# Convolution layer's two projections by seven half-size products per pair of column blocks, on one core

## What is computed

```
h = rms_norm(x, norm_g) @ w_in                  # w_in: 2048 x 8192
b_gate, c_gate, hx, z = split(h, 4)
u = c_gate * hx
conv = causal width-3 convolution of u, per channel
y = (b_gate * conv * silu(z)) @ w_out           # w_out: 2048 x 2048
x = x + y
```

## Time and profile before

| | |
|---|---|
| time, median of 3 runs | 2505.37 us (2504.8 to 2506.09) |
| span of the profiled execution | 2504.4 us |
| PE busy | 2451.6 us (98%) |
| DVE busy | 1500.7 us (60%) |
| ACT busy | 1020.4 us (41%) |
| first product of `conv_in` | at 33.12 us |
| first matmul of `project_and_score` (block 0) | at 1004.63 us |
| first matmul of its block 1 | at 1018.52 us |

### The profile page before, as it was taken

How to read it: one execution, slowest core, us unless ns; L and a number is a source line. 1 busy time by engine, 2 the same in 40 slices (tenths; PEclk the granted TensorE clock), 3 DMA queues, 4 the chain that set the end, 5 groups by cost and what they waited for, 6 DMA issues and landing times.

```text
span 2504.4 us, 51142 instructions
## 1 busy us (share of the span) xinstructions
PE 2451.6 (98%) x20963; PEld 2152.2 (86%) x20963; DVE 1500.7 (60%) x1682; ACT 1020.4 (41%) x1848; POOL 341.4 (14%) x134
## 2 busy tenths in 40 slices
PE   8999999999999999999999999999999989899998
PEld 7999999999999999999999989999999833355555
DVE  5675556566666334455699887777677567533311
ACT  4111112111112223677745468777645445531111
POOL 4423332332321011000000000000000013300000
PEclk9999999999999999999999999999999999999999
DMA  5333332333332433322577777787889899999997
GB/s 159 85 84 93 91 84 84 84 84 86 99 84 69 122 106 108 104 99 90 189 266 268 254 260 257 248 295 271 289 292 307 296 372 416 402 345 374 388 410 299
DMA packets 361063, 520.54 MB, mean 208 GB/s; under 512 B 17033, under 2 KB 289810, under 8 KB 342418
## 3 DMA queue, kind: packets, MB, share of 16 engines
q1 hardware_dynamic: 304578, 461.55, 53.4%
q10 hardware_dynamic: 56192, 56.45, 6.5%
q0 software_dynamic: 128, 0.26, 0.0%
HBM read 483.46 MB, written 34.75 MB: 207 GB/s over the span
## 4 chain that ended last, share of the span: by engine, by line
PE 86%; DVE 4%; ACT 4%; DMA 3%; issue 1%; SPq 1%; POOL 0%; ACTq 0%; DVEq 0%; POOLq 0%
PE psum L117 25%; PE psum L1311 17%; PE psum L125 13%; PE psum L1319 8%; PE psum L2015 7%; PE psum L1362 4%; PE psum L2094 4%; DMA w_raw<-in_w_in_b_dram 2%; DVE h_keys_turned L1254 1%; PE psum L2073 1%; ACT w_raw L1075 1%; PE psum L1327 1%; PE psum L2054 1%; DMA w_raw<-in_w_in_a_dram 1%; PE psum L1341 1%
## 5 line engine op out<-in xcount | busy, mean ns | idle before, releaser
L1311 PE MATMUL psum<-x_hi,w_hi 128*128 128x272 f32 x2048 | 433.4, 293 | 0.8 <-ACT work L133 0.8
L117 PE MATMUL psum<-x_hi,w_hi 128*128 128x272 f32 x2048 | 426.7, 289 | 2.2 <-DVEq L451 2.2
L117 PE MATMUL psum<-x_lo,w_hi 128*128 128x272 f32 x2048 | 425.8, 289 | 0.0
L1311 PE MATMUL psum<-x_lo,w_hi 128*128 128x272 f32 x2048 | 424.9, 289 | 0.0
L1311 PEld LDWEIGHTS psum<-x_hi,w_hi 128*128 128x128 f32 x2048 | 321.2, 189 | 17.7 <-issue 17.6
L117 PEld LDWEIGHTS psum<-x_hi,w_hi 128*128 128x128 f32 x2048 | 321.1, 189 | 2.7 <-issue 2.3
L1311 PEld LDWEIGHTS psum<-x_lo,w_hi 128*128 128x128 f32 x2048 | 321.0, 188 | 0.0
L117 PEld LDWEIGHTS psum<-x_lo,w_hi 128*128 128x128 f32 x2048 | 320.5, 188 | 0.0
L1254 DVE STREAM_TRANSPOSE h_keys_turned<-h_ring 128x1024 f32<-128x1024 f32 x256 | 300.0, 1215 | 21.3 <-DMA h_ring<-in_cache_k_dram 12.3
L404 POOL TENSOR_TENSOR w_raw<-w_raw,params 128x2048 f32<-128x2048 f32 x63 | 243.4, 3864 | 504.5 <-DMA w_raw<-in_w_in_a_dram 504.5
L1319 PE MATMUL psum<-x_hi,w_lo 128*128 128x272 f32 x2048 | 284.1, 294 | 0.0
(11 more groups left out here) (222 smaller groups left out, 2987.5 us busy)
## 6 DMA issues: line engine op xcount, KB each, us to landing
h_ring<-in_cache_k_dram SPq DMA_DIRECT2D x256, 512.0 KB, 6.4
ring<-in_cache_v_dram SPq DMA_DIRECT2D x128, 1024.0 KB, 7.7
w_raw<-in_w_in_a_dram SPq DMA_DIRECT2D x64, 1024.0 KB, 6.2
w_raw<-in_w_kv_dram SPq DMA_DIRECT2D x16, 2048.0 KB, 13.2
w_raw<-in_w_in_b_dram SPq DMA_DIRECT2D x15, 2048.0 KB, 8.9
w_raw<-in_w_out_a_dram SPq DMA_DIRECT2D x16, 1024.0 KB, 5.6
wo_raw<-in_w_out_b_dram SPq DMA_DIRECT2D x32, 512.0 KB, 7.8
ring<-in_w_out_b_dram SPq DMA_DIRECT2D x16, 1024.0 KB, 6.6
```

The lines of the kernel that those rows point to most:

```text
L117: pe.matmul(out[:, g, 0:GT], m.WH[s][:, k * P:(k + 1) * P], x[:, k * T + g * GT:k * T + (g + 1) * GT], start=(k == 0 and x is xh), stop=Fa ...
L1311: pe.matmul(psum[n % 2][:, g, 0:GT], m.WH[n % 2][:, k * P:(k + 1) * P], x[:, k * T + g * GT:k * T + (g + 1) * GT], start=(k == 0 and x is ...
```

## The change

One function, `seven_products`, takes the place of `read_inputs`, `conv_in` and `conv_out`. It takes two column blocks at a time, so 40 steps (n = 0 to 39; 32 for `w_in`, 8 for `w_out`). A step's weights are cut into four quarters A11, A12, A21, A22 (even or odd row tiles, first or second block; 8 tiles of 128x128 each), and the activations into quarters likewise (even or odd channel tiles, first or second group of 272 columns). By Strassen's scheme (in Winograd's form) the four quarters of the result come of seven products of half size in place of eight, numbered mm = 0 to 6, with the left sides A11, S1, S2, A12, S3, A22, S4, where S1 to S4 are sums of quarters. A product is 16 matmuls with the high half of its left side and 8 with the low half, each 128x128 by 272 columns, all into one PSUM bank. The first product's bank is copied by ACT into another bank (`seed`) and two later products add to that; ACT and DVE take the quarters out (`take_u2`, `take_u3`, `take_quarter`, `gather`).

Per step, DVE makes the four sums (1024 columns each) and seven low halves, ACT seven high halves. SP loads the four quarters apart, 512 KB each in pieces of 512 bytes.

The seven right sides are the quarters of x and their sums. In step 0 they are made from x, which is now multiplied by the norm weight on ACT while it is turned (so the weights of `w_in` are no longer scaled), and raw x is stored to memory. For `w_out` the right sides are made from y, step by step; they are stored to memory in `conv_extras` (they don't fit beside those of x) and loaded again during step 31 by `load_right`: 14 transfers of 128 rows of 7616 bytes, on ACT's queue. From step 32 to 39, x is added back, split, and the split halves are stored, and during step 39 loaded again by `load_x1` into `x_hi` and `x_lo`, but for the last two tiles: six transfers of 128 rows of 8704 bytes and two of 4352. The first two weight blocks of the next stage are loaded by SP after product 3 of step 39 (2 MB in pieces of 512 bytes). The gate's SiLU is one ACT instruction. The additions of squares in the last 8 steps stay on POOL. All loops are written out.

DVE at the start, before: for each of the first channel tiles the low half of x, and for odd tiles the sum of squares.

The diff, cut:

```diff
--- before.py
+++ after.py
-def project_hi(pe, m, s, out, xh, xl, waits={}):
...
-def project_lo(pe, m, s, out, xh):
...
-def load_next(sp, m, following, lo_ready, raw_in, n):
...
+IN_STEPS, OUT_STEPS = 2 * KT, KT // 2
+STEPS = IN_STEPS + OUT_STEPS
+TICKS = STEPS * PRODUCTS
+LEFT = ["A11", "S1", "S2", "A12", "S3", "A22", "S4"]
+RIGHT = [0, 4, 1, 2, 3, 5, 6]
+BANK_OF = [0, 2, 1, 0, 1, 6, 2]
...
+OPENS = (0, 1, 5)
...
+        return {"S2": 0, "S3": 1, "S1": 4, "S4": 5 + n % 2, "A21": 8, "A22": (9, 7)[n % 2], "A11": 10, "A12": 11}[name]
...
+            def load(name, n):
+                kind, i, part = columns_of(n)
+                w, col = (d["w_in_a"][0], CONV_IN_COLS[part] + 2 * i * P) if kind == "in" else (d["w_out_a"][0], 2 * i * P)
+                if name == "A21" and n:
+                    sp.wait_ge(s_ready, 4 * (n - 1) + 3)
+                if name == "A22" and n >= 2:
+                    sp.wait_ge(product_done, PRODUCTS * (n - 2) + 6)
+                if name == "A22" and n == 1:
+                    sp.wait_ge(xt_ready, KT)
+                if name == "A11" and n:
+                    sp.wait_ge(product_done, PRODUCTS * (n - 1) + 1)
+                if name == "A12" and n:
+                    sp.wait_ge(product_done, PRODUCTS * (n - 1) + 4)
+                sp.sem_inc(granted, 1)
+                odd, right = int(name[2]) - 1, int(name[1]) - 1
+                sp.dma_start(arena.left(name, n).rearrange("p (k c) -> p k c", k=EDGE),
+                             w.rearrange("(k two p) c -> two p k c", two=2, p=P)[odd][:, :, col + right * P:col + (right + 1) * P]
+                             ).then_inc(w_in[name], 16)
...
+            sp.wait_ge(s_ready, 4 * STEPS)
+            sp.wait_ge(product_done, PRODUCTS * LAST + 4)
+            for s in range(SLOTS):
+                sp.sem_inc(granted, 1)
+                sp.dma_start(tiles(m.RAW[s][:, :]), w_block(w, cols + s * P)).then_inc(q_in[s], 16)
+            for s in range(SLOTS):
+                sp.wait_ge(q_in[s], 48 - 16 * s)
...
+                if k == 0:
+                    act.wait_ge(par_ready, 1)
+                act.wait_ge(raw_ready, k + 1)
+                if k % 2 == 0:
+                    both = arena.plain[0][:, :].rearrange("p (o x) -> p o x", x=RW)[:, 4:8:3, :]
+                    act.activation(both[:, :, i * GT:(i + 1) * GT], xt, ACT.Copy, scale=gain).then_inc(gx_ready, 1)
+                else:
+                    act.activation(arena.right_plain(2)[:, i * GT:(i + 1) * GT], xt[:, 0, :], ACT.Copy, scale=gain)
+                    act.activation(arena.right_plain(6)[:, i * GT:(i + 1) * GT], xt[:, 1, :], ACT.Copy, scale=gain).then_inc(gx_ready, 1)
+                after(act, sq_used, k - 1)
+                act.activation(grouped(sq[k % 2][:, :]), xt, ACT.Square).then_inc(sq_ready, 1)
+                if k >= 1:
+                    x_raw_store(k - 1)
...
+            def split_high(q):
+                if q >= TICKS:
+                    return
+                n, mm = divmod(q, PRODUCTS)
+                left_landed(act, LEFT[mm], n)
+                after(act, product_done, q - 3)
+                act.activation(arena.left_high(q), arena.left(LEFT[mm], n), ACT.Copy).then_inc(hi_ready, 1)
...
+                act.activation(arena.right(order, 0), arena.right_plain(order), ACT.Copy).then_inc(right_high, 1)
...
+                act.wait_ge(product_done, PRODUCTS * n + 1)
+                if n == 0:
+                    act.wait_ge(seed_bits, 1)
+                if n >= 2:
+                    act.wait_ge(product_done, PRODUCTS * (n - 2) + 5)
+                act.activation(bank(n, 2), bank(n, 0), ACT.Copy).then_inc(act_took, 1)
...
+                    act.activation(b1, b2, ACT.Silu).then_inc(act_gate, 1)
...
+            def load_right(mm):
+                order = RIGHT[mm]
+                act.wait_ge(product_done, PRODUCTS * (IN_STEPS - 1) + mm + 1)
+                if mm == 0:
+                    act.wait_ge(y_out, 80 * (EDGE - 1))
+                entry = [0, 4, 1, 5, 3, 6, 2][order]
+                for low in range(2):
+                    act.dma_start(arena.right(order, low)[:, 0:(EDGE - 1) * GT].bitcast(F32),
+                                  st.YS[low, entry].rearrange("p i t -> p (i t)")[:, 0:(EDGE - 1) * GT]).then_inc(right_in[mm], 16)
...
+                if n == LAST and mm in (1, 3, 4):
+                    load_x1({1: 0, 3: 1, 4: 2}[mm])
+                if n == LAST and mm == 6:
+                    load_x1(3)
...
+            def load_x1(order):
+                act.wait_ge(product_done, PRODUCTS * LAST + RIGHT.index(order) + 1)
+                if order == 3:
+                    x1_stored(act, OUT_STEPS - 2)
+                k0, k1 = 4 * order, (4 * order + 4 if order < 3 else KT - 2)
+                for low, x in enumerate((XH, XL)):
+                    act.dma_start(x[:, k0 * T:k1 * T].bitcast(F32), st.X1S[low][:, k0 * T:k1 * T]).then_inc(right_in[order], 16)
...
+            act.wait_ge(q_in[1], 32)
+            for k in range(KT):
+                wk = m.RAW[1][:, k * P:(k + 1) * P]
+                ins = act.activation(wk, wk, ACT.Copy, scale=m.PAR[:, following[2] + k:following[2] + k + 1])
+            ins.then_inc(q_scaled, 1)
+            act.wait_ge(q_scaled, 2)
+            act.wait_ge(product_done, PRODUCTS * LAST + 4)
+            act.activation(m.WH[0][:, :], m.RAW[0][:, :], ACT.Copy).then_inc(q_high, 1)
...
+                    done = k // 4 * 3
+                    dve.wait_ge(gx_ready, k + 1)
+                    dve.tensor_tensor(t1, b12, b11, ALU.subtract).then_inc(t_step, 1)
+                    dve.wait_ge(t_step, done + 1)
+                    dve.tensor_tensor(t2, b22, t1, ALU.subtract).then_inc(t_step, 1)
+                    dve.tensor_tensor(b12, b22, b12, ALU.subtract)
+                    dve.wait_ge(t_step, done + 2)
+                    dve.tensor_tensor(t4, b21, t2, ALU.subtract).then_inc(t_step, 1)
...
+            def gather(n, mm):
+                dve.wait_ge(product_done, PRODUCTS * n + (2, 6, 7)[mm])
+                if mm == 0:
+                    dve.wait_ge(act_took, 4 * n + 4)
+                    dve.tensor_tensor(quarter(n, 1, 1), u3, bank(n, 1), ALU.add).then_inc(dve_took, 1)
+                if mm == 1:
+                    dve.tensor_tensor(quarter(n, 1, 0), u3, bank(n, 5), ALU.add).then_inc(dve_took, 1)
+                if mm == 2:
+                    dve.tensor_tensor(quarter(n, 0, 1), u2, bank(n, 6), ALU.add).then_inc(dve_took, 1)
...
+                if n == 0 and mm < 5:
+                    right_lows(2 + mm)
+                if n + 1 < STEPS and mm >= 3:
+                    (sum_1, sum_2, sum_3, sum_4)[mm - 3](n + 1)
...
+            dve.wait_ge(q_high, 1)
+            dve.wait_ge(product_done, PRODUCTS * LAST + 5)
+            dve.tensor_tensor(m.WL[0][:, :], m.RAW[0][:, :], m.WH[0][:, :].bitcast(F32), ALU.subtract).then_inc(q_low, 1)
+            gather(LAST, 2)
+            add_x(OUT_STEPS - 1)
+            x1_lows(OUT_STEPS - 1)
...
+                for k in range(EDGE):
+                    if n == IN_STEPS and k == EDGE - 1:
+                        pe.wait_ge(right_high, PRODUCTS + mm + 1)
+                        pe.wait_ge(yl_ready, 2 * (EDGE - 1) + mm + 1)
+                    for low in range(2):
+                        pe.matmul(to, wh[:, k * P:(k + 1) * P], arena.right(RIGHT[mm], low)[:, k * GT:(k + 1) * GT],
+                                  start=(mm in OPENS and k == 0 and low == 0), stop=False, skip_group_check=True)
+                pe.wait_ge(lo_ready, q + 1)
+                for k in range(EDGE):
+                    last = pe.matmul(to, wl[:, k * P:(k + 1) * P], arena.right(RIGHT[mm], 0)[:, k * GT:(k + 1) * GT],
+                                     start=False, stop=(k == EDGE - 1), skip_group_check=True)
+                last.then_inc(product_done, 1)
...
@@ build @@
-                one = read_inputs(nc, m, d, st, (d["w_in_a"][0], CONV_IN_COLS[0:2]), block)
...
-                conv_in(nc, m, d, st, (d["w_out_a"][0], 0), one, block)
-                conv_out(nc, m, d, st, head_weights(d, "q"), one, block)
+            one = seven_products(nc, m, d, st, Arena(plain, rounded), extra, extra_r, head_weights(d, "q"), block)
```

1131 lines of the change are left out of this document (680 added, 451 removed).

## The result

The changed kernel takes **2447.95 us** (median of 4 runs, 2445.57 to 2451.49) beside 2505.68 us (2504.8 to 2506.09) for the kernel before on the same chip: a ratio of **0.9773, 95% interval 0.9759 to 0.9787**. The gain is 57.7 us, where 42 was forecast. (The 2505.37 us above are the median of the first three of the kernel before's four runs here.) The profiled execution has a span of 2446.5 us.

What follows compares the result with a forecast made beforehand. PE was taken as bound by the first layer's matmul count. From 2504.4 us: -120.6 matmuls, -2 a wait, +31.6 start, +18 and +31 the two turns give a span of 2462.4; forecast 2463 us, range 2424 to 2497.

Steps and rivals of the forecast that it cites:

- What bounds the kernel: In the first layer PE is bound by its number of matmuls; each one removed is worth its pitch.
- an eighth of the matmuls: Over the 40 steps 960 matmuls go, at 0.1256 us each: -120.6 us; no change of pitch taken.
- The steady steps hide their new work: In steps of 21.09 us, DVE's and ACT's added work stays hidden under PE: no cost.
- 90%, under PE: DVE's work over four steps of `w_in`: 76 of 84.4 us, so hidden under PE.
- It fits, by 0.4 us: At a third step's start, ACT's seed copy ends at 5.6 us, before product 2 begins at 6.0.
- The start: Before steady steps, DVE and ACT hand over in turn: first product at 56 us, step 0 ends at 89; +31.6 us.
- The turn to the second projection: Around steps 31 and 32, left side A12 lands late beside large right-side packets: +16 us, +18 with PE's clock.
- Products 5 and 6 find their right sides landed: At the turn to the second projection, these products of step 32 wait for no right sides: no cost.
- 2 us for PE's clock: After the wait at the second projection, PE starts again at 1.2 GHz: about 2 us.
- The turn to the next stage: After step 39, weight blocks land late behind x's transfers; block 1 starts 45.3 us after step 39: +31 us.
- turn 1: The turn to the second projection, steps 31 and 32: forecast at +18 us.
- turn 2: The turn to the next stage, from the last step's start to block 1: forecast at +31 us.

Runs made afterwards that it cites:

- e6: Changed kernel with 24 more matmuls in each step's last product, as many as before the change (projection values wrong): 2567.5 us.
- e12: Changed kernel with one more DVE instruction per product in steps 1 to 31, which nobody waits for: 2491.12 us.
- e5: Changed kernel with POOL adding only 16 of 544 columns of each tile's squares at the start (norm wrong): 2443.68 us.
- e7: Changed kernel with the 14 loads of right sides on SP's queue, in one row with the left sides in due order: 2450.47 us.
- e9: As e7, with the left side A12 of step 32 loaded ahead of the third pair of right sides: 2447.7 us.
- e8: Changed kernel with x1's loads and the next stage's weight blocks in due order on SP's queue, and ACT rounding the first block before scaling the second: 2434.94 us.
- e1: Changed kernel with the second projection's right sides padded in memory, so loads go in packets of 1088 bytes instead of 7616: 2458.03 us.
- e10: Changed kernel with the edits of e8 and e9, and the start's sums made after the next four tile copies: 2433.36 us.
- e3: Changed kernel with ACT rounding the next stage's first weight block before scaling the second: 2446.68 us.

## Why the prediction was right

**The range and the sign held, and the forecast was 15 us too slow.** Three of its sums are right in their mechanism and near in size, one is near in size by luck, and the largest miss lies where it had no term. Point by point:

- *What bounds the kernel* and *an eighth of the matmuls*: right. 3.01 us per product, 0.1255 per matmul, no price for one bank (as the earlier trace rows had pointed to). e6 gives the count of matmuls as the gain of the steps.
- *The steady steps hide their new work*: right, at 21.09 us, and durations as worked out. The transposes of the last rows, 0.2 us in every fourth step, were not counted. The sentence "90%, under PE" was made over four steps (85% measured, 71.3 of 84.4); e12 shows that the hand-overs and the fullest steps decide. The line that mattered was "It fits, by 0.4 us": the copy behind `first_tap` was forecast to end at 5.6 us of the third step and ends at 5.4, and it is the place where e12 first makes PE wait. In a kernel a little fuller the 90% would have misled.
- *The start*, 31.6 forecast and 28.9 measured: the mechanism is right (DVE and ACT in turn, rounds of 10.0 us where 10.8 was worked out), the first product at 53.9 where 56 was named. ACT's 1.75 us per tile was too much: the issue of a store runs beside its instructions, and a tile takes 1.2 to 1.4 us. The contention, +1.3 per round, was too little: 1.9. The Trainium skill ("SBUF — State Buffer", section "Who interferes with whom") has a VectorE operation with both inputs in SBUF and a GpSimd one shut each other out. e5 agrees: 1.6 and 1.74 us beside POOL, 0.72 without.
- *The turn to the second projection*, 18 forecast and 14.8 measured: **the step that failed is the cause, and the near number is luck.** It was A11 of step 32 that starved first, in step 31, not A12, and only 2.5 of the 14.8 us lie at product 0, where all 16 were put. "Products 5 and 6 find their right sides landed" left out another 6.1 us, for which PE waited on DVE, behind left sides that had landed late. e7 and e9, in which all these loads stand in one queue in due order, cost 12.2 to 12.5, within the scatter of kernels without an edit there. The bytes are the bound, and the working had them in it (4.7 us per pair, "isn't empty from 7.5 to about 42") without drawing the sum. The 2 us for PE's clock were read from the matmuls before 36 us in the kernel before. Their pitch there is double, 0.226 us, but the profile's granted clock is 1.00; in after the clock did fall in this turn, to 0.81 and 0.68. (A slip in the sum: 39.3 and 1.2 are 40.5, not 40.3.)
- *The turn to the next stage*, 31 forecast and 30.3 measured: each link is there. The second block landed at 38.1 after the last step's start (41.2 forecast), block 0 started at 44.9 (48.3), block 1 at 65.3 (66.4). Block 0 itself took 20.5 us where 18.1 were forecast, since PE ran it at half its clock at first (0.50 from 949 to 955 us), so two misses of 2 to 3 us met. e8 proves the link by taking 14.4 us out of it.
- *Not in the prediction at all*: the 9.2 us of the later stages, the largest single miss, of which 1.0 is explained. It is over half of the 15.9 us between the forecast span and the measured one, the rest being start 2.7, turn 1 3.2, turn 2 0.7, and 2.0 of waits of the layer before that were not counted as saved, less 1.9 of steps.

## What to carry to other kernels

When loads pile up at a turn, add up the bytes that are due by each date before asking who starves whom: where nearly all are due at once, neither packet size nor order helps (e1, e7, e9), and where the full queue holds what is due later, one queue in due order gave back 14 us (e8). Smaller packets share better but cost the issuing engine its time; issue them from an engine that has none to lose. And measure an engine's room at the hand-overs of its fullest steps, not over a round of steps: 3.8 us per step added to an engine that is busy for 82 to 85% cost 43 us, where the sum of its work was over full by 0.5 us per step.

## What the runs showed of the hardware

- An engine that issues transfers with many packets can be held in the issue: 952 KB per issue took ACT 0.3 to 1.0 us in packets of 7616 bytes, and in packets of 1088, from the fourth issue on, 2.4 to 3.6. From 750 to 756 us all queues moved 369 GB/s and ACT's 250, at which one such transfer takes 2.6 and 3.9 us, so that the issue went about as fast as the queue drained; that it waits for room in the queue is inferred.
- Two busy queues gave each other packet for packet whatever the sizes: 684 of 7616 bytes against 690 of 512, 1411 of 1088 against 1411 of 512.
- Twenty-four matmuls of 272 columns into one bank keep the pitch of alternating groups, 0.1255 us.
- In e8 PE stood still for 10.3 us; its granted clock was at half, 1.2 GHz, from 928 us on, and still in the first 4 us of its new work. When it falls again differs between nearly equal kernels: after a wait of 2.8 us it was at half in e10 from 938 to 944 us, after one of 2.9 in e8 at full. In step 0 the clock is at half for 3 us too, in after from 75 to 78 us and in e3 from 84 to 87 (0.54), and step 0 takes 32.5 or 34.0 us in these kernels, with no edit that would change it.
- The same code, run behind a changed layer, took 3 to 10 us less in 1480, of which 1.0 is explained.
